# The RWKV recurrence of a two-block transformer kernel as a three-stage software pipeline over token blocks, both heads together

## What is computed

```
def step(state, inp):
    r_t, w_t, k_t, v_t, a_t, b_t = inp
    sa = einsum('bhvk,bhk->bhv', state, a_t)
    state = state * w_t + sa (x) b_t + v_t (x) k_t
    y = einsum('bhvk,bhk->bhv', state, r_t)
    return state, y
```

## Time and profile before

| what | value |
|---|---|
| median of three runs | 2790.9 us (2789.16 to 2795.78) |
| profiled execution, span | 2791.3 us |
| TensorE, VectorE, ScalarE, GpSimd busy | 97%, 50%, 45%, 44% |
| recurrence | from about 766 to 1235 us |
| TensorE's granted clock in the whole execution | 0.997 |

### The profile page before, as it was taken

One profiled execution on the slowest core, in us unless ns is written; L12 is line 12 of the kernel. 1 busy time (PEld: TensorE's weight loads), 2 busy tenths in 40 slices (PEclk: granted clock), 3 DMA queues, 4 the chain that ended last, 5 costly groups with the idle time before them and its releaser, 6 DMA issues.

```text
span 2791.3 us, 55493 instructions
## 1 busy us (share of the span) xinstructions
PE 2697.6 (97%) x23340; PEld 2154.4 (77%) x23340; DVE 1402.7 (50%) x2503; ACT 1264.0 (45%) x2292; POOL 1233.6 (44%) x1145
## 2 busy tenths in 40 slices
PE   8999999989999999989999999999999999999999
PEld 6678888867778888777888877587777777788887
DVE  6847885055667777754888022612223333244410
ACT  5754443234666666544444235634444453422221
POOL 5234444546733433325444446054443645544443
PEclk9999999999999999999999999999999999999999
DMA  5112332322300000103332322032222322323222
GB/s 177 42 54 91 93 96 91 94 95 91 90 16 6 8 8 8 36 29 98 91 98 87 96 88 76 12 114 74 76 77 69 100 74 91 98 91 98 89 90 78
DMA packets 67079, 208.64 MB, mean 75 GB/s; under 512 B 14736, under 2 KB 15376, under 8 KB 66448
## 3 DMA queue, kind: packets, MB, share of 16 engines
q1 hardware_dynamic: 63680, 192.96, 22.5%
q0 software_dynamic: 2576, 10.78, 1.1%
q10 hardware_dynamic: 576, 1.35, 0.1%
HBM read 199.69 MB, written 4.19 MB: 73 GB/s over the span
## 4 chain that ended last, share of the span: by engine, by line
PE 88%; DVE 6%; ACT 2%; POOL 2%; issue 2%; DMA 0%; SPq 0%; DVEq 0%; ACTq 0%; POOLq 0%
PE banks L1803 22%; PE banks L1805 22%; PE banks L1804 22%; PE banks L826 6%; PE banks L835 1%; PE banks L1975 1%; PE banks L943 1%; POOL low L321 1%; PE banks L819 1%; PE banks L2037 1%; PE banks L2023 1%; PE banks L892 1%; DVE low L550 1%; PE banks L2012 1%; DVE arena L2842 1%
## 5 line engine op out<-in xcount | busy, mean ns | idle before, releaser
L321 POOL TENSOR_TENSOR low<-arena,high 128x256 fp32r<-128x256 f32 (+3 forms) x817 | 967.7, 1207 | 1149.8 <-ACT high L309 1149.7
L1803 PE MATMUL banks<-high,high 128*128 128x512 f32 (+1 forms) x2728 | 1080.8, 396 | 10.9 <-DVE arena L2706 2.9
L1805 PE MATMUL banks<-high,low 128*128 128x512 f32 (+1 forms) x2728 | 1070.5, 392 | 0.0
L1804 PE MATMUL banks<-low,high 128*128 128x512 f32 (+1 forms) x2728 | 1070.1, 392 | 0.0
L309 ACT ACTIVATE high<-arena 128x1024 fp32r<-128x1024 f32 (+1 forms) x376 | 382.1, 1016 | 799.3 <-PE banks L1805 797.7
L1803 PEld LDWEIGHTS banks<-high,high 128*128 128x128 f32 x2728 | 513.5, 188 | 139.2 <-issue 5.5
L1805 PEld LDWEIGHTS banks<-high,low 128*128 128x128 f32 x2728 | 513.4, 188 | 119.6
L1804 PEld LDWEIGHTS banks<-low,high 128*128 128x128 f32 x2728 | 513.7, 188 | 117.8 <-issue 1.9
L2740 DVE TENSOR_TENSOR arena<-banks,arena 128x512 f32<-128x512 f32 x48 | 33.1, 692 | 424.4 <-PE banks L1805 423.3
L2871 DVE SCALAR_TENSOR_TENSOR arena<-arena 128x511 f32<-128x511 f32 x88 | 237.2, 2695 | 3.1
L826 PE MATMUL banks<-arena 64*64 64x64 f32 x5632 | 200.3, 222 | 17.6 <-ACT arena L1204 10.7
(11 more groups left out here) (319 smaller groups left out, 3079.4 us busy)
## 6 DMA issues: line engine op xcount, KB each, us to landing
arena<-weights SPq DMA_DIRECT2D x301, 512.0 KB, 3.5
arena<-weights SPq DMA_DIRECT2D x48, 448.0 KB, 3.3
arena<-weights SPq DMA_DIRECT2D x28, 256.0 KB, 2.6
arena<-tables POOLq DMA_DIRECT2D x5, 448.0 KB, 3.6
arena<-x_t SPq DMA_DIRECT2D x4, 512.0 KB, 5.8
x_spill<-arena POOLq DMA_DIRECT2D x1, 2048.0 KB, 9.4
arena<-x_spill POOLq DMA_DIRECT2D x1, 2048.0 KB, 8.8
out_t<-arena SPq DMA_DIRECT2D x8, 256.0 KB, 4.1
```

The costliest lines, as they stand in the source:

```text
L321: low = pool.tensor_tensor(lo[:, part], ring[w % RING][:, part], hi[:, part].bitcast(F32), ALU.subtract)
L1803: pe.matmul(dst, hi[:, c], x[0], start=kt == 0, stop=False)
L1804: pe.matmul(dst, hi[:, c], x[1], start=False, stop=False)
L1805: mm = pe.matmul(dst, lo[:, c], x[0], start=False, stop=kt == kts_of[t] - 1)
```

## The change

Pass i now holds three stages on three solves: the growing half of solve i (scores, squares 1 to 3, grow 2 and 3), the second half of solve i - 1 (grow 4, both merges, tokens) and the state of i - 2. There are 34 passes. Both heads go together in every product and every copy: one semaphore step, one ScalarE or VectorE instruction of double width. U is no longer grown by VectorE's additions: a unit is added to each power instead (W2 on GpSimd, W4 and W8 on VectorE), and ScalarE copies the product, which is the new U. The merges keep VectorE's sums. R.AM and R.U have three buffers, R.NM two; R.U's two first lie in the space of x, so the load of x_spill is split, and its first eighth comes after the recurrence. `split_low` of the late weight piece moves there too. Small tiles move. The turned masks share banks PJ with the scores.

ScalarE's order in a pass: copy of grow 4 (i-1); side; merge 1 (i-1); SA 0 (i-2); side; outputs 0; square 1; merge 2 (i-1); square 2; SA 1; side (with a table load in c = 0; the one of c = 2 stands before merge 1's copy); grow 2; outputs 1; grow 3; tokens (i-1); side.

VectorE's side pieces move within the pass. By pass c, in the slots first / masks / state / powers / last: c = 0: y_bonus, sum floor, rkk, kk, y_normed; c = 1: first half of the decay sums, y_out, second half with the three chunk sums, centre, exclusive; c = 2: the same of the other direction one slot earlier each (decay; decay and chunk sums; centre and exclusive), then z_gate, y_mean; c = 3: y_average, y_centre, r_ and a_, y_square and y_var, r_ and a_. On GpSimd k_a and b_k stood behind U1 of their pass; they now stand behind U1 and W2.

```diff
-    R.AM = [at(o + 768 * i, 2, 2, 3 * C) for i in range(2)]; o += 2 * 768
+    R.AM = [at(o + 768 * i, 2, 2, 3 * C) for i in range(3)]; o += 3 * 768
-    R.U = [at(o + 256 * i, 2, 2, C) for i in range(2)]; o += 512
+    R.U = [at(XAT, 2, 2, C), at(XAT + 256, 2, 2, C), at(o, 2, 2, C)]; o += 256
-    R.NM = at(o, 2, 3, P); o += 768
+    R.NM = [at(o + 512 * i, 2, 2, P) for i in range(2)]; o += 1024
...
-        def product(bank, col, lhs, rhs, flip=0):
-            for q in range(2):
-                for p in range(2):
-                    mm = pe.matmul(bank[hf(p ^ flip), col + C * q:col + C * q + C], lhs(hf(p), q), rhs(hf(p), q), start=True, stop=True)
-            return mm
...
+        def both(into, col, lhs, rhs, rows_in, rows_out):
+
+            row = {"even": lambda p, h: hf(p), "turned": lambda p, h: hf(p ^ h)}
             for q in range(2):
                 for p in range(2):
                     for h in range(2):
-                        last[h] = pe.matmul(into[h][hf(p ^ h), col + C * q:col + C * q + C], lhs(hf(p), h, q), rhs(hf(p), h, q),
+                        r, to = row[rows_in](p, h), row[rows_out](p, h)
+                        mm = pe.matmul(into[h][to, col + C * q:col + C * q + C], lhs(r, h, q), rhs(r, h, q), start=True, stop=True)
...
+        def square(i, s):
             if s == 1:
-                d2.wait(pe, i, f"D_{h}")
-                m, mt = (lambda r, q: R.D[r, h, q, :]), half_of(R.NM, h, 0)
+                md.wait(pe, i, "D")
+                m, mt, way = lanes_of(R.D), half_of(R.P4, 1), ("even", "even")
             else:
-                a2.wait(pe, i, f"S{s - 1}_{h}")
+                ga.wait(pe, i, f"S{s - 1}")
                 src = R.P2 if s == 2 else R.P4
-                m, mt = half_of(src, h, 0), half_of(src, h, 1)
+                m, mt, way = half_of(src, 0), half_of(src, 1), ("even", "turned") if s == 2 else ("turned", "even")
+            mm = both(PJ, 0, mt if s < 3 else m, m if s < 3 else mt, *way)
             if s < 3:
...
+        def grow(i, s):
+            u = lanes_of(R.U[i % 3])
+            if s == 2:
+                if i:
+                    mb.wait(pe, i - 1, "U6")
+                gg.wait(pe, i, "W2")
+                mm = both(PI, 0, lanes_of(R.D), u, "even", "turned")
+            elif s == 3:
+                gd.wait(pe, i, "W4")
+                ga.wait(pe, i, "U2")
+                mm = both(PI, 0, half_of(R.P2, 0), u, "turned", "even")
             else:
+                gd.wait(pe, i, "W8")
+                ga.wait(pe, i, "U3")
+                mm = both(PI, 0, half_of(R.P4, 0), u, "even", "even")
...
+            both(PI, 0, half_of(R.NM[i % 2], m - 1), u, "even", "turned")
+            mp.inc(both(PI, P, u, unit, "even", "turned"), f"Q{m}")
+
+        def merged(i, m):
+            ma.wait(pe, i, f"Q{m}")
+            mp.inc(both(PI, 2 * P, half_of(R.Q, 1), half_of(R.Q, 0), "turned", "even"), f"U{m + 4}")
...
+        for i in range(ITERS + 2):
+            growing, merging, seq = i < ITERS, 0 < i <= ITERS, i > 1
+            if merging:
+                grow(i - 1, 4)
+            if growing:
+                turned_scores(i)
+            if seq:
+                solve(i - 2, 0)
+            side(i, "state 0")
+            if merging:
+                merge(i - 1, 1)
+            if growing:
                 scores(i)
+            if merging:
+                merged(i - 1, 1)
             if seq:
+                advance_state(i - 2, 0)
+                second_state(i - 2, 0)
+            if i == ITERS + 1:
+                gate(KT - 2, psum[2])
+            if growing:
+                square(i, 1)
+            if seq:
+                read_state(i - 2, 1)
+            if merging:
+                merge(i - 1, 2)
+            if growing:
+                square(i, 2)
+            if seq:
+                solve(i - 2, 1)
+            if merging:
+                merged(i - 1, 2)
+            if i == ITERS + 1:
+                gate(KT - 1, psum[3])
+            side(i, "merged")
+            if growing:
+                square(i, 3)
+            if seq:
+                advance_state(i - 2, 1)
+                second_state(i - 2, 1)
+            if growing:
+                grow(i, 2)
+            if merging:
+                tokens(i - 1)
+            if growing:
+                grow(i, 3)
+            side(i, "grown")
+            if merging:
                 read_state(i - 1, 0)
...
-                d2.wait(pool, i, f"D_{h}")
-                g2.inc(pool.tensor_tensor(R.U[i % 2][:, h, :, :], R.D[:, h, :, :],
-                                          eye.unsqueeze(1).to_broadcast([P, 2, C]), ALU.add), f"U1_{h}")
             if c == 0:
                 k_sum(j)
+            md.wait(pool, i, "D")
+            gg.inc(pool.tensor_tensor(R.U[i % 3], R.D, eyes, ALU.add), "U1")
+            gg.wait(pool, i, "U1")
+            ga.wait(pool, i, "S1")
+            gg.inc(pool.tensor_tensor(R.D, R.P2[:, :, 1, :].rearrange("p h (q c) -> p h q c", q=2), eyes, ALU.add), "W2")
...
+        def mask_turned(i):
+            sp.wait(dve, i, "NT")
+            md.inc(dve.tensor_tensor(R.NM[i % 2], both_j[:, :, 0:P].unsqueeze(2).to_broadcast([P, 2, 2, P]),
+                                     below[:, 1:3, :].unsqueeze(1).to_broadcast([P, 2, 2, P]), ALU.mult), "N")
+            md.inc(dve.tensor_tensor(turned_masks(), both_j[:, :, 0:P], below[:, 0, :].unsqueeze(1).to_broadcast([P, 2, P]),
+                                     ALU.mult), "DT")
+
+        def mask_lanes(i):
+            sp.wait(dve, i, "A")
+            md.inc(dve.tensor_tensor(R.AM[i % 3], four[:, :, :, C:4 * C], lanes.unsqueeze(1).to_broadcast([P, 2, 2, 3 * C]),
+                                     ALU.mult), "M")
+
+        def mask_diagonal(i):
+            md.inc(dve.tensor_tensor(R.D, four[:, :, :, 0:C], diag.unsqueeze(1).to_broadcast([P, 2, 2, C]), ALU.mult), "D")
+
+        def add_merged(i, s):
+            mp.wait(dve, i, f"U{s}")
+            u = R.U[i % 3].rearrange("p h q c -> p h (q c)")
+            mb.inc(dve.tensor_tensor(u, both_i[:, :, 2 * P:3 * P], u, ALU.add), f"U{s}")
+
+        def add_values(it, q):
+            if q == 0:
...
+        for i in range(ITERS + 2):
+            growing, merging, seq = i < ITERS, 0 < i <= ITERS, i > 1
+            spread(i, "first")
+            if growing:
+                mask_turned(i)
+            spread(i, "masks")
+            if growing:
+                mask_lanes(i)
             if seq:
+                new_state(i - 2, 0)
+            if merging:
+                add_merged(i - 1, 5)
+            if growing:
+                mask_diagonal(i)
             if seq:
+                add_values(i - 2, 1)
+            spread(i, "state")
+            if merging:
+                add_merged(i - 1, 6)
+            if growing:
+                ga.wait(dve, i, "S2")
+                with_unit(R.P2[:, :, 0, :], R.P4[:, :, 1, :], "W4")
+                gp.wait(dve, i, "S3")
+                with_unit(R.P4[:, :, 0, :], both_j[:, :, 0:P], "W8")
+            spread(i, "powers")
             if seq:
+                new_state(i - 2, 1)
+            spread(i, "last")
+            if merging:
+                add_values(i - 1, 0)
```

More of the change, by code:

```diff
@@ L780, in side @@
                     od.wait(pe, j - 2, "y")
-                gate(j - 2, bank, 0)
-            elif at_ == (2, "last sum") and j >= 2:
-                gate(j - 2, bank, 1)
-            elif at_ == (2, "merge 2"):
+                gate(j - 2, bank)
+            elif at_ == (2, "grown") and j < KT:
                 if j >= 2:
@@ L789, in side, with turned_scores @@
                 bonus(j, bank)
[L790 removed]
+            elif at_ == (3, "state 0") and j:
                 ba.wait(pe, j, "bon")
                 turn_y(j - 1, "bt", bank)
[L793 to L797 removed]
+        def turned_scores(i):
             j, c = i // TT, i % TT
@@ L989, in pe_rwkv @@
                 scores(i)
+            if merging:
+                merged(i - 1, 1)
             if seq:
-                read_state(i - 1, 0)
-            if i == ITERS:
-                gate(KT - 2, psum[2])
-            if off:
-                side(i, "masks")
-                square(i, 0, 1)
-                square(i, 1, 1)
-            if seq:
-                solve(i - 1, 0)
-            if off:
-                for s in (2, 3):
-                    for h in range(2):
-                        square(i, h, s)
-                        grow(i, h, s)
@@ L1005, in pe_rwkv @@
-            if seq:
-                advance_state(i - 1, 0)
-            if off:
-                tokens(i, 0)
-            if seq:
-                second_state(i - 1, 0)
-            if off:
-                tokens(i, 1)
-                grow(i, 0, 4)
-                grow(i, 1, 4)
-            if seq:
-                read_state(i - 1, 1)
-            if i == ITERS:
-                gate(KT - 1, psum[3])
-            if off:
-                side(i, "last sum")
```

(24 more changed lines are left out.)

555 lines of the change are left out of this document (242 added, 313 removed).

## The result

The kernel after takes 2845.2 us (median of 4 runs, 2843.1 to 2846.2) against 2791.3 for the kernel before on the same chip (4 runs): ratio 1.0187, 95% interval 1.0172 to 1.0201. It is 54 us slower; I had forecast 22. The sign was right, the size not, and 2845 lies above my range. So a gain given as a difference of two medians can be off by 2 us, and two ratios with intervals of 0.15% to either side differ clearly only from some 0.2%, 6 us, on.

The account below looks back on a forecast made before the run. TensorE's own work was taken to bound the recurrence. Savings of 90 us against 75 us of new waits gave 2776; 37 us of collisions made it 2813 us, +22, with a range of 2765 to 2840.

Parts of the forecast that it names:

- The wait for D: Square 1 needs D, late in VectorE's new order: TensorE stands still 1.5 us a pass, +48 us.
- The widths of instructions: Durations of wider instructions: VectorE 0.42, 0.67, 0.93 us for 256, 512, 768 columns; ScalarE 0.60, 0.81 for 512, 768.
- The collisions: VectorE and GpSimd hold each other up on SBUF in GpSimd's new place: 5.8 us per head group, +37 us in all.
- The fourth pass: Fourth pass of a head group: six VectorE instructions meet four b_k of 1.27 us, costing 3.0 us.
- The second: Second pass of a head group: three tiny chunk sums each wait for one k_a instruction, costing 2.8 us.
- Rival 3: Every VectorE-GpSimd meeting costs the whole instruction and the last b_k holds the next scores: 2844 us; 0.10 shared with another rival.
- The four corners: Squares 2 and 3, grow 2 and 3: 80 records a pass, each 14.4 ns cheaper, 1.15 us a pass, -37 us.
- The tail: 34 passes for 33: the new last but one takes about 8 us, the first two are lighter by 3, +5.
- The small waits: New TensorE waits: square 2 for ScalarE's copy +6, scores for the turned masks +8, solve for X +8 us.
- waits for ScalarE that were to go: Weight loads' waits for ScalarE's copies, mostly between a merge and its second product, filled with other work: -30 us.
- The clock: Stalls of 1.5 us several times a pass may bring a second window of lower clock; a few us at most.
- what should show it: Signs: under 20 ns a record, D's wait largest at 45 us, long chunk sums, alternating passes, VectorE's busy time falling little.

Follow-up runs that it names:

- e2_pool_early: Kernel after, with GpSimd's first k_a of a head group and first b_k moved ahead of U1: 2817.3 us, ratio 1.0083 to the kernel before.
- e1_d_early: Kernel after, with VectorE masking D right behind the lane masks, before the state and addition U5: 2813.8 us, ratio 1.0068 to the kernel before.

## Why the prediction was half right

**The wait for D (+48): right.** The weight loads of line 846 wait 49.0 us for line 1693 in all, and taking two thirds of it away gave 31 us back. The working by neighbours' durations held: 1.5 us a pass forecast, 1.4 measured.

**The widths of instructions: right.** 0.958 for 768 columns (0.93 reckoned), 0.689 for 512 (0.67), 0.414 for 256 (0.42); ScalarE 0.597 and 0.806 (0.60 and 0.81).

**The collisions (+37): about right in sum, right in one of two places.** 30 to 34 us by lightening, 28 by moving half the work, 2 in the kernel before (I had deducted 4). The fourth pass was right: 3.0 us forecast, and it fell by 2.9 and 3.0. The second was not: 2.8 forecast, and it fell by 0.9 and 0.5, since the chunk sums lose 0.7 us and not 2.8. What makes up for it in the sum I had not counted: the first pass of a head group fell by 0.4 to 0.5, and in both runs TensorE was busy less with the same records (12 and 7 us) at a higher granted clock. That the sum agrees is in part luck. The Trainium skill (SBUF — State Buffer, "SBUF: two separate sides") has it that a VectorE instruction with two SBUF inputs and a GpSimd instruction that reads SBUF lock each other out for the whole instruction; 0.859 us in the mean and 0.414 without a meeting, for the same addition of line 1678, agrees. Rival 3 gives nearly the measured time, 2844, but not for its reason: it asks 68 us of the collisions and a wait for the last b_k, and the runs show about half of that and a wait for a_. Its number is luck.

**The four corners (-37): the step that failed.** "One record is thus 14.4 ns dearer" holds (14.0). What failed is the line after it, that 80 such records are 1.15 us of every pass. That is the price where TensorE bounds the stretch, as it did before; but the same text has TensorE waiting for VectorE at D, at W8 and at X. A gain on the engine that has just been put behind another's waits is mostly more waiting: 11 us in this kernel, 17 to 19 with the waits relieved. This is 26 of the missing 32 us.

**The tail (+5): the second failed step.** I counted the extra pass's products and took ScalarE's, VectorE's and GpSimd's other work there for hidden. The tail grew by 15.6 us; 8 to 10 of that went when such work stepped aside. In the passes TensorE has other stages' products to run while a copy is late; in the two last passes it has not, and the instructions ahead of a copy make the tail longer. The 29.6 us that are left then are 6.5 more than before, near the 8 that I had put for the extra pass. The 3 us that the first two passes were to be lighter by did not come: they take 29.9 us, and 29.4 before.

With both steps mended, 22 + 26 + 11 = 59 against 54 measured. The small waits were under the size forecast: square 2 for ScalarE's copy 4.3 us (6), the scores for the turned masks 2.4 (8), solve for X 0.8 in the passes (8; the prediction's own factors, 0.8 in 8 passes, make 6.4). Of the 30 us of waits for ScalarE that were to go, 23 went.

**The clock: not counted, and partly open.** I called it a few us. Of the passes of the kernel after, 51 us ran at 1.2 GHz, none of the kernel before; 14 of them lie in the first pass and most of the rest at the end of a fourth one (from 1073 to 1081 us the granted clock is 0.60; it fell within the 2.75 us of idle time above). The same records keep TensorE busy 390 us there and 379 in `e2_pool_early`, at 0.98: some 12 us of work, of which it is not known how much lay on the path. It came back with GpSimd's work moved, and not with the wait for D gone, where the clock is still 0.95. So the collisions and the clock are not cleanly apart, and neither is the clock's part in the 54 us.

Of what should show it: the four corners' records did, 62 of them (merge 2 and square 2) in 1.36 us with their result, so some 18 ns each behind the first result:

```profile
1065.37 1.36 PE L846 MATMUL banks<-arena 64*64 64x64 f32 x62
```

The wait for D and the long sums did; VectorE's busy time did not fall at all; the passes by kind were 15.2, 15.4, 13.9 and 18.2 us, so one kind, not two, stands out.

## What to carry to other kernels

Work out a saving on an engine only after the waits that the same change adds to it: if it now waits, the saving is idle time, and the order of the engine that it waits for is what to tune. When the work of a pass is reordered, look at what now runs side by side on VectorE and GpSimd from SBUF, not only at what waits for what. At the end of a pipeline nothing covers a late copy, so instructions that are not the chain's belong behind it there.

## What I had not expected of the hardware

An 8-column copy on VectorE (line 1536), which has one SBUF input only, took 0.171 us in seven passes in which GpSimd ran nothing, and 0.52 to 1.05 in the seven in which an instruction of GpSimd was under way; it ended each time within 0.05 us of that instruction's end. So a tiny instruction loses what is left of the other's. A 128x256 addition ranged from 0.414 to 1.93 us, the longest beside a GpSimd instruction of 2.37. And the granted clock did not follow TensorE's idle time: 0.95 over the passes with 92 us idle (the kernel after), 0.97 with 73 (on two corners), 0.98 with 75 (`e2_pool_early`), but 0.95 with 61 (`e1_d_early`).
